# Final layer normalisation of a mixture-of-experts step: its work divided anew between VectorE, ScalarE and Pool

## The reference, cut to what matters

```python
def _layernorm(x, g, b):
    xf = x.astype(jnp.float32)
    mu = jnp.mean(xf, -1, keepdims=True)
    var = jnp.mean(jnp.square(xf - mu), -1, keepdims=True)
    return ((xf - mu) * lax.rsqrt(var + LN_EPS) * g + b).astype(x.dtype)
...
x = _layernorm(DEEPNORM_ALPHA * x + mix, ln1_g, ln1_b)
x = _layernorm(DEEPNORM_ALPHA * x + _moe(x, ...), ln2_g, ln2_b)
```

## Time and profile before

| what | value |
|---|---|
| median of 3 runs | 1702.13 us |
| lowest and highest | 1701.24, 1702.68 us |
| span of the profiled execution | 1703.1 us |
| VectorE busy | 819.5 us (48%) |
| ScalarE busy | 663.1 us (39%) |
| Pool busy | 236.0 us (14%) |

### The profile page before, as it was taken

The page is one execution under the profiler, slowest core; times in us unless marked ns, Lnnn a source line. Parts: engine busy times, 40 slices in busy tenths (PEclk is TensorE's granted clock), DMA queues, the critical chain, the costliest instruction groups (busy, mean ns, idle before and its releaser), DMA issues. The chain is left out here.

```text
span 1703.1 us, 25703 instructions
## 1 busy us (share of the span) xinstructions
PE 1601.3 (94%) x9847; PEld 1464.5 (86%) x9847; DVE 819.5 (48%) x1362; ACT 663.1 (39%) x1117; POOL 236.0 (14%) x292
## 2 busy tenths in 40 slices
PE   7999999999999999999999999999998599999980
PEld 7988898889989898999999999999787488888760
DVE  3433463353033433313032323233647799999975
ACT  5422241222254554522112111112212488888866
POOL 1000120013011111130000000000000254443220
PEclk9999999999999999999999999999998699999995
DMA  6111231125211112062325124111432899999736
GB/s 183 40 38 38 73 112 49 36 66 167 78 48 41 68 44 79 19 188 79 126 62 179 46 66 143 38 38 67 162 132 81 278 265 273 326 300 290 190 60 230
DMA packets 154225, 204.34 MB, mean 120 GB/s; under 512 B 14723, under 2 KB 121235, under 8 KB 154104
## 3 DMA queue, kind: packets, MB, share of 16 engines
q1 hardware_dynamic: 135224, 140.82, 26.3%
q0 software_dynamic: 18880, 61.89, 13.1%
HBM read 152.34 MB, written 50.34 MB: 119 GB/s over the span
## 5 line engine op out<-in xcount | busy, mean ns | idle before, releaser
L380 PE MATMUL ps<-xh,slab_hi 128*128 128x384 f32 (+1 forms) x504 | 171.8, 341 | 1.4 <-DVE slab_lo L732 1.4
L380 PE MATMUL ps<-xh,slab_lo 128*128 128x384 f32 (+1 forms) x504 | 165.1, 328 | 0.0
L380 PE MATMUL ps<-xl,slab_hi 128*128 128x384 f32 (+1 forms) x504 | 165.0, 327 | 0.0
L1899 PE MATMUL ps<-xh,slab_lo 128*128 128x384 f32 (+1 forms) x384 | 125.2, 326 | 0.0
L1899 PE MATMUL ps<-xh,slab_hi 128*128 128x384 f32 (+1 forms) x384 | 125.1, 326 | 0.0
L1899 PE MATMUL ps<-xl,slab_hi 128*128 128x384 f32 (+1 forms) x384 | 125.1, 326 | 0.0
L2100 DVE TENSOR_TENSOR gt_sg<-ps,gt_sg 128x384 f32<-128x384 f32 (+1 forms) x48 | 25.7, 536 | 186.5 <-PE ps L1899 186.3
L380 PEld LDWEIGHTS ps<-xh,slab_hi 128*128 128x128 f32 x504 | 95.0, 188 | 15.4 <-issue 13.6
L2869 PE MATMUL ps<-mo_hi_gu,mo_xh 128*128 128x512 f32 x256 | 100.3, 397 | 0.9 <-ACT mo_xh L2972 0.7
L2869 PE MATMUL ps<-mo_hi_gu,mo_xl 128*128 128x512 f32 x256 | 98.9, 391 | 0.0
L2040 ACT ACTIVATE gt_sg<-ps 128x384 f32<-128x384 f32 (+1 forms) x48 | 22.7, 473 | 191.1 <-PE ps L1899 191.1
(11 more groups left out here) (500 smaller groups left out, 4219.3 us busy)
## 6 DMA issues: line engine op xcount, KB each, us to landing
slab_raw<-in_w_in SPq DMA_DIRECT2D x60, 512.0 KB, 4.2
mo_raw_g<-in_w_e_gate SPq DMA_DIRECT2D x16, 1024.0 KB
mo_raw_u<-in_w_e_up SPq DMA_DIRECT2D x16, 1024.0 KB
mo_raw_d<-in_w_e_down SPq DMA_DIRECT2D x16, 1024.0 KB
gt_oh<-oT_hi SPq DMA_DIRECT2D x3, 2176.0 KB, 7.8
gt_ol<-oT_lo SPq DMA_DIRECT2D x3, 2176.0 KB, 12.7
slab_raw<-in_w_branch SPq DMA_DIRECT2D x24, 256.0 KB, 4.6
x_dram<-slab_raw SPq DMA_DIRECT2D x9, 512.0 KB, 5.1
```

The costliest lines, as they stand in the source:

```text
L380: mm = eng.matmul(out, w[:, b, k, :], x[:, k, t0:t0 + tn], start=(k == 0 and j == 0), stop=(k == KC - 1 and j == 2), skip_group_check=True)
L1899: last = eng.matmul(out, w[:, s % 2, c, wk, :], x[:, k, t0:t0 + tn], start=(k == 0 and i == 0), stop=(k == ks[-1] and i == 2))
```

## The change

Four things change in the final normalisation.

- The statistics of tiles 0 and 4 are made by VectorE: two bn_stats over 512 columns each and one bn_aggr that gives mean and variance. ScalarE skips those tiles, and takes only the square root of their variance, between its mean and its squares of the next tile.
- The last step of tiles 0, 1, 3, 4, 6 and 7 is made by Pool in two instructions: a tensor_scalar that multiplies the centred tile by the reciprocal in place, a wait on its own semaphore `scaled`, and a tensor_tensor that adds `bb` and writes `total(t)`. VectorE keeps the single instruction for tiles 2, 5 and 8.
- Centred tiles go in turn to four buffers, two of `mo_y` and two of `mo_xg`. Before VectorE writes one that Pool has used, it waits for Pool's result of four tiles earlier.
- SP waits for Pool's or VectorE's semaphore, whichever makes the tile, still in the order of the tiles.

VectorE's order becomes: statistics of 0; then for each tile centre, the statistics of the next tile if it is tile 4, reciprocal, and shift if the tile is 2, 5 or 8. It also waits once for the last transposes of the rows (`x_tr`) and no longer waits for its own shift of a tile before it starts the next.

```diff
+        STATS_BY_VECTOR = (0, 4)
+        SHIFT_BY_VECTOR = (2, 5, 8)
+        SHIFT_BY_POOL = (0, 1, 3, 4, 6, 7)
+        def centred(t):
+            return (y[:, 0, :], y[:, 1, :], xg[:, 2, :], xg[:, 3, :])[t % 4]
+        def freed(eng, t):
+            if t >= 4 and t - 4 in SHIFT_BY_POOL:
+                eng.wait_ge(pool_out, SHIFT_BY_POOL.index(t - 4) + 1)
...
             for t in range(NT):
-                eng.wait_ge(o_ready, t + 1)
+                if t in SHIFT_BY_POOL:
+                    eng.wait_ge(pool_out, SHIFT_BY_POOL.index(t) + 1)
+                else:
+                    eng.wait_ge(o_ready, SHIFT_BY_VECTOR.index(t) + 1)
...
+            eng.wait_ge(c_in, 32)
+            for n, t in enumerate(SHIFT_BY_POOL):
+                eng.wait_ge(rstd_ready, t + 1)
+                eng.tensor_scalar(centred(t), centred(t), rstd[:, t:t + 1], None, ALU.mult).then_inc(scaled, 1)
+                eng.wait_ge(scaled, n + 1)
+                eng.tensor_tensor(total(t), centred(t), bb, ALU.add).then_inc(pool_out, 1)
...
             for t in range(NT):
                 c = slice(t, t + 1)
+                if t in STATS_BY_VECTOR:
+                    continue
...
+                if t - 1 in STATS_BY_VECTOR:
+                    eng.wait_ge(var_ready, STATS_BY_VECTOR.index(t - 1) + 1)
+                    eng.activation(std[:, t - 1:t], mv[:, t - 1, 1:2], ACT.Sqrt, bias=small[:, :]).then_inc(std_ready, 1)
+                eng.wait_ge(mean_ready, means_by_scalar(t))
...
+            def statistics(t):
+                eng.wait_ge(t_in[t], 16)
+                for half in range(2):
+                    ch(eng.bn_stats(st[:, half, :], total(t)[:, 512 * half:512 * half + 512]))
+                ch(eng.bn_aggr(mv[:, t, :], st[:, :, :].rearrange("p a n -> p (a n)")))
+                eng.sem_inc(var_ready, 1)
+            def centre(t):
+                c = slice(t, t + 1)
+                freed(eng, t)
+                if t in STATS_BY_VECTOR:
+                    ch(eng.scalar_tensor_tensor(out=centred(t), in0=total(t), scalar=mv[:, t, 0:1], in1=gb,
+                                                op0=ALU.subtract, op1=ALU.mult))
...
+            def inverse(t):
+                c = slice(t, t + 1)
                 eng.wait_ge(std_ready, t + 1)
-                ch(eng.reciprocal(rstd[:, c], std[:, c]))
-                eng.scalar_tensor_tensor(out=total(t), in0=y[:, t % 2, :], scalar=rstd[:, c], in1=bb,
-                                         op0=ALU.mult, op1=ALU.add).then_inc(o_ready, 1)
+                eng.reciprocal(rstd[:, c], std[:, c]).then_inc(rstd_ready, 1)
...
+            statistics(0)
             for t in range(NT):
-                normalise(t)
-                eng.wait_ge(o_ready, t + 1)
+                centre(t)
+                if t + 1 in STATS_BY_VECTOR:
+                    statistics(t + 1)
+                inverse(t)
+                if t in SHIFT_BY_VECTOR:
+                    eng.wait_ge(rstd_ready, t + 1)
+                    eng.scalar_tensor_tensor(out=total(t), in0=centred(t), scalar=rstd[:, t:t + 1], in1=bb,
+                                             op0=ALU.mult, op1=ALU.add).then_inc(o_ready, 1)
```

More of the change, by code:

```diff
@@ L2740, in stage_experts, with means_by_scalar @@
         small = sb("small", [128, 1])
+        st, mv = sb("st", [128, 2, 6]), sb("mv", [128, NT, 2])
+        var_ready, rstd_ready, scaled, pool_out = sem("var_ready"), sem("rstd_ready"), sem("scaled"), sem("pool_out")
         gb, bb = xg[:, 0, :], xg[:, 1, :]
+        STATS_BY_VECTOR = (0, 4)
+        SHIFT_BY_VECTOR = (2, 5, 8)
+        SHIFT_BY_POOL = (0, 1, 3, 4, 6, 7)
+        def means_by_scalar(t):
+            return len([u for u in range(t + 1) if u not in STATS_BY_VECTOR])
+        def centred(t):
[3 more added lines that the diff above has]
+                eng.wait_ge(pool_out, SHIFT_BY_POOL.index(t - 4) + 1)
         def total(t):
@@ L3032, in _ @@
                 eng.activation(negmean[:, c], total_of[:, c], ACT.Copy, scale=-1.0 / D).then_inc(mean_ready, 1)
-                eng.wait_ge(mean_ready, t + 1)
+                if t - 1 in STATS_BY_VECTOR:
+                    eng.wait_ge(var_ready, STATS_BY_VECTOR.index(t - 1) + 1)
+                    eng.activation(std[:, t - 1:t], mv[:, t - 1, 1:2], ACT.Sqrt, bias=small[:, :]).then_inc(std_ready, 1)
+                eng.wait_ge(mean_ready, means_by_scalar(t))
                 ch(eng.activation(sh.ps[:, 0:2, :].rearrange("p a n -> p (a n)"), total(t), ACT.Square, bias=negmean[:, c],
@@ L3116, in _ @@
             ch = Chain(eng, co_dve)
-            def normalise(t):
-                c = slice(t, t + 1)
[L3120 to L3123, removed]
+            def statistics(t):
[4 more added lines that the diff above has]
+                eng.sem_inc(var_ready, 1)
@@ new lines, in centre @@
+            def centre(t):
+                c = slice(t, t + 1)
+                freed(eng, t)
+                if t in STATS_BY_VECTOR:
+                    ch(eng.scalar_tensor_tensor(out=centred(t), in0=total(t), scalar=mv[:, t, 0:1], in1=gb,
+                                                op0=ALU.subtract, op1=ALU.mult))
+                else:
+                    eng.wait_ge(mean_ready, means_by_scalar(t))
+                    eng.wait_ge(t_in[t], 16)
+                    ch(eng.scalar_tensor_tensor(out=centred(t), in0=total(t), scalar=negmean[:, c], in1=gb,
+                                                op0=ALU.add, op1=ALU.mult))
@@ L3124, in normalise @@
+            def inverse(t):
+                c = slice(t, t + 1)
                 eng.wait_ge(std_ready, t + 1)
-                ch(eng.reciprocal(rstd[:, c], std[:, c]))
-                eng.scalar_tensor_tensor(out=total(t), in0=y[:, t % 2, :], scalar=rstd[:, c], in1=bb,
-                                         op0=ALU.mult, op1=ALU.add).then_inc(o_ready, 1)
+                eng.reciprocal(rstd[:, c], std[:, c]).then_inc(rstd_ready, 1)
             eng.wait_ge(c_in, 32)
+            eng.wait_ge(x_tr, 2 * NTILE)
```

## The result

The changed kernel takes 1717.65 us (median; 1716.42 to 1718.25) against 1702.09 us for the kernel before beside it: ratio 1.0087 with an interval of 1.0075 to 1.0099, slower by 0.87%. The forecast was 1714.9 us, slower, with a range of 1700 to 1719. The profiled execution has a span of 1716.6 us, 13.5 us over that of before, while the median grew by 15.6 us. The two profiles aren't equally typical of their kernels: most times of both kernels lie 1.6 to 1.7 us above the span of the same execution (here 1718.25 against 1716.6), so a span isn't its execution's time. The profiled execution before, with its span of 1703.1 us, was by this estimate about 2.7 us slower than the median of its kernel.

What follows compares the result with a forecast made beforehand. The prediction took the SBUF read interface shared by VectorE and Pool as the bound: 1673.8 + 36.1 + 2.1 = 1712.0, plus 3.9 us closing, less 1.0 for the median, gives 1714.9 us; range 1700.0 to 1719.0.

Steps and rivals of the forecast that it cites:

- What bounds, and the load of ScalarE and VectorE: Final part: ScalarE and VectorE share one load almost evenly; after the change 20.7 us and 20.9 us.
- the equal paces: Final part before the change: VectorE 2.87 us a tile, ScalarE 2.89, so relieving one alone brings almost nothing.
- Exclusion: VectorE's two-SBUF-input instructions and Pool's SBUF reads take turns, each for its whole length; chance 0.70, 1714.9 us.
- The 37 indirect DMAs: Expert stage: of 64, those starting inside a two-SBUF-input VectorE instruction end 0.81 to 0.87 or 1.42 to 1.50 us after it.
- the column-by-column rival: Final part: the interface is held only for columns read, 28.2 us in turn, end at 1707.0 us; chance 0.10.
- Pool's price: Pool's 1024-column multiplication 1.10 us, addition 2.3 us (1.04 to 2.75); six tiles of 3.4 us make 20.4 us.
- The sum: Read interface from 1673.8: 36.1 us of work, 2.1 us idle, last writer at 1712.0; with the closing, 1714.9 us.
- The rival on the other side: No exclusion for streams: Pool runs freely beside VectorE, 1700.9 us, 1.2 us faster; chance 0.17.
- The closing: After the last writer: tile 7 and sample rows stored together, 3.4 us as before plus 0.5 us for another issue.
- Signs: Changed profile: VectorE up to 3.6 us or late, ScalarE idle 5 us, last deviation near 1699, Pool last near 1712.

Runs made afterwards that it cites:

- stats_only: Changed kernel without its Pool part: VectorE makes all nine shifts and still the statistics of tiles 0 and 4; 1704.01 us, ratio 1.0001 to before.
- psum_gain: Changed kernel with gain and shift copied once into PSUM for VectorE's centrings and shifts; 1711.83 us, ratio 1.0044 to before.
- pool_last: Kernel before plus one Pool fill of 128 columns that waits for VectorE's last shift; 1704.99 us, ratio 1.0023 to before.
- split4_psum: Changed kernel with gain and shift in PSUM, Pool's multiplication as tensor_tensor, Pool tiles 0, 2, 4, 6, VectorE statistics 0, 3; 1699.42 us, ratio 0.9988.
- split4_early: split4_psum with Pool's tiles 0, 2, 3 and 5 in place of 0, 2, 4 and 6; 1702.11 us, ratio 1.0000 to before.

## Why the prediction was right, and where it was not

**What bounds, and the load of ScalarE and VectorE: right.** Moving two tiles' statistics from ScalarE to VectorE brought nothing by itself (stats_only), as the equal paces said.

**Exclusion: right in kind.** The 37 indirect DMAs of the kernel before had shown it, and psum_gain confirms it by taking it away. I took the whole instruction as its length. For Pool's addition that is right to 0.19 us; for its multiplication it is wrong, 0.77 to 0.91 of 2.84 us. Those are near the 0.85 us of 1024 columns at the 0.834 ns of the earlier trace rows, but the addition's 2.00 to 2.15 us are more than two such passes, and no VectorE instruction got in ahead of the last 0.19 us of an addition, so the column-by-column rival isn't what happens either. The Trainium skill (SBUF — State Buffer, section SBUF: two separate sides) has whichever instruction starts first keep the interface for the whole instruction, and the multiplication's 0.77 to 0.91 us disagree. The Trainium skill (SBUF — State Buffer, section Who interferes with whom) also says that a VectorE instruction with at most one input in SBUF doesn't collide with Pool, and psum_gain's 1.28 us agree.

**Pool's price: the step that failed.** The addition measured 2.34 us (2.3 assumed). The multiplication measured 2.84 us, where I took 1.10 and had 1.8 as the upper end. The range varied the price of the addition alone and kept 1.10 for the multiplication. I had also excluded that the addition could cost less than the multiplication, since it moves no less; it costs 0.5 us less. I had read a fill and a select as the price of any instruction with one input; they are the price of a copy (1.03 us). The Trainium skill (GPSIMD Engine Reference, section When to use GPSIMD) calls instructions with one input roughly line-rate; the copy agrees and the tensor_scalar's 2.84 us do not.

**The sum: right by luck, with errors that cancelled.** I had the interface as the bound: it starts 5.0 us after the first load's issue, has 36.1 us of holds and 2.1 us idle, and the last writer ends 1712.0 - 1668.8 = 43.2 us after that issue; measured 43.4. In truth the bound is Pool: it starts 6.9 us after the issue and has 31.5 us of own work and 5.1 us of waits. Pool's own work was taken 31.5 - 20.4 = 11.1 us too low. The holds come to about 32.0 us, 4.1 less than forecast, and the 2.1 us of idle time didn't come (Pool's queue was full when the statistics of tile 4 were made). All this met in nearly the same number, since the wrong resource was added up. With the true prices and whole-instruction holds the same sum would have given 15.7 + 31.5 = 47.2 us of holds and, even without idle time, 1673.8 + 47.2 + 3.9 - 1.0 = 1723.9 us, above the range. The size of the forecast is no proof of its working.

**The rival on the other side couldn't have come.** I gave 0.17 to no exclusion and 1700.9 us. psum_gain is that case and is 0.44% slower than before, about 1709.6 us on the scale of 1702.1: with the true price of the multiplication six tiles on Pool are too many whatever the interface does. The lower part of the range rested on the price of 1.10 us.

**The closing: mis-sized.** I had 3.9 us (two stores together) and it was 5.5. A Pool instruction that ends late closes the program 5.5 us after it by itself (pool_last), while the sample rows had landed 3.5 us after their issue at 1711.50. The forecast was 2.75 us low: 0.2 us is the stage, 1.6 the closing, and 2.05 that the median lies 1.05 us above the profiled span now where it lay 1.0 below before; against these, the first load was issued 1.1 us earlier.

**Signs.** VectorE's instructions lasted up to 3.36 us (forecast 3.6), Pool's addition of tile 7 was last, ScalarE was idle 3.3 us ahead of its root of tile 4 (forecast 5) and its last deviation came at 1696.0, not near 1699, since VectorE reached tile 4 earlier than I had it.

## What to carry to other kernels

Before work goes to Pool, take each instruction's price from a run of that very instruction: on this chip a multiplication of 1024 columns by a per-row value took 2.84 us on Pool, a copy 1.03. Look at VectorE's instructions beside it: with two inputs in SBUF they and Pool wait for each other, and moving one operand to PSUM removed every such wait at a cost of 2.5 us (two copies of 1.23) in a stretch where VectorE was idle anyway. In the runs here a third engine paid only where its whole queue ended before VectorE's last work (split4_psum, 0.12%), and with in-order stores each of its tiles must be ready in time for the tiles behind it (split4_early, no gain). A sum that meets the measured time can still have added up the wrong engine; check each term against its row.

## What the runs showed of the hardware

- Pool, 128x1024 f32, alone: tensor_scalar 2.84 us, tensor_tensor 2.34, tensor_tensor with a spread per-row value 1.89, copy 1.03.
- Pool's tensor_scalar keeps a VectorE instruction with two SBUF inputs out for its first 0.77 to 0.91 us of 2.84; a tensor_tensor until 0.19 us before its end. While VectorE's instruction is in, Pool's waits for its end.
- An indirect DMA issued on Pool inside such a VectorE instruction waits for its end too: in the kernel before 17 additions took 2.67 us on average against 1.57 for the 14 free ones, 20 gathers 2.18 against 0.98 for 12.
- Where a Pool instruction came last, the span ended 5.5 to 5.7 us after its end, even where no one uses its result (pool_last); before, it ended 3.4 us after VectorE's last shift. The cause isn't known.
